# A two-layer backbone step: the second split pair of input projections taken half by half, and the bias load placed behind two weight loads

## What is computed

```python
sh1, sc1, g1, sh2, sc2, g2 = modulation(cond, w_ada[l], b_ada[l])   # silu(cond) @ w_ada, 6144 columns
h = rms_norm(x, norm1_g) * (1 + sc1) + sh1
proj = jnp.dot(h, w_in)
q_lat, ckv_raw, krope, conv_in, na_qkv = jnp.split(proj, IN_SPLITS, axis=-1)
...
s_loc = jnp.where(in_win, s_loc + bias, NEG_INF)    # neighbourhood attention, learned bias rpb
p = jax.nn.softmax(jnp.concatenate([s_loc, s_ctx], axis=-1), axis=-1)
...
x = x + g1 * jnp.dot(mix, w_out)
x = x + g2 * grouped_moe(h2, w_router, b_router, w_gate, w_up, w_down)
```

## Time and profile before

| | us |
|---|---|
| median of three runs | 1145.73 |
| lowest and highest run | 1142.65, 1146.65 |
| the profiled execution | 1150.03 |
| its span | 1148.2 |
| what lies around the span | 1.83 |

### The profile page before, as it was taken

How to read it: one execution, slowest core, us unless ns; L and a number is a source line. 1 busy time by engine, 2 the same in 40 slices (tenths; PEclk the granted TensorE clock), 3 DMA queues, 4 the chain that set the end, 5 groups by cost and what they waited for, 6 DMA issues and landing times.

```text
span 1148.2 us, 14862 instructions
## 1 busy us (share of the span) xinstructions
PE 1083.5 (94%) x5616; PEld 863.0 (75%) x5616; DVE 880.1 (77%) x1075; ACT 703.2 (61%) x927; POOL 227.0 (20%) x212
## 2 busy tenths in 40 slices
PE   5899799999899999999999999989889999999996
PEld 2677456588777888888878976778778888888884
DVE  1368554574899999998976688766689999899894
ACT  2334165553487887888855346653378788887880
POOL 2201411010323212212101033201215121221100
PEclk9899899989999999999999998969999999999998
DMA  9867696844689999999971323104599999999971
GB/s 380 321 257 278 199 378 263 312 187 170 263 340 361 356 394 377 375 389 378 388 296 53 112 106 106 48 1 202 196 345 375 355 389 380 382 357 378 379 290 56
DMA packets 54266, 320.63 MB, mean 279 GB/s; under 512 B 11610, under 2 KB 11722, under 8 KB 19248
## 3 DMA queue, kind: packets, MB, share of 16 engines
q1 hardware_dynamic: 38448, 276.59, 62.5%
q0 software_dynamic: 15744, 43.05, 10.1%
HBM read 313.37 MB, written 25.44 MB: 295 GB/s over the span
## 4 chain that ended last, share of the span: by engine, by line
PE 74%; DVE 15%; DMA 4%; ACT 3%; issue 3%; POOL 1%; SPq 0%; DVEq 0%; POOLq 0%; ACTq 0%
PE bank L1278 39%; PE bank L899 6%; PE bank L1170 5%; DVE w_lo L2436 5%; PE bank L917 4%; PE bank L882 3%; DMA ring<-wring_dram 3%; PE bank L994 3%; PE bank L1029 3%; PE bank L960 2%; PE bank L1270 2%; PE bank L927 1%; PE bank L1351 1%; PE bank L1307 1%; ACT probs L1564 1%
## 5 line engine op out<-in xcount | busy, mean ns | idle before, releaser
L2436 DVE TENSOR_TENSOR w_lo<-ring,w_hi 128x2048 fp32r<-128x2048 f32 x192 | 436.5, 2289 | 39.7 <-ACT w_hi L1715 39.6
L1715 ACT CAST w_hi<-ring 128x2048 fp32r<-128x2048 f32 x192 | 367.1, 1918 | 36.9 <-PE bank L1278 36.8
L1278 PE MATMUL bank<-w_hi,hgT_hi 128*128 128x512 f32 x512 | 202.3, 395 | 6.1 <-issue 4.2
L1278 PE MATMUL bank<-w_hi,hgT_lo 128*128 128x512 f32 x512 | 199.9, 391 | 0.0
L1278 PE MATMUL bank<-w_lo,hgT_hi 128*128 128x512 f32 x512 | 199.7, 390 | 0.0
L810 POOL DMA_INDIRECT y_rows<-y,y_at x26 | 48.2, 1852 | 354.4 <-ACT y L1746 325.4
L1278 PEld LDWEIGHTS bank<-w_hi,hgT_hi 128*128 128x128 f32 x512 | 96.2, 188 | 26.8 <-issue 7.7
L1278 PEld LDWEIGHTS bank<-w_hi,hgT_lo 128*128 128x128 f32 x512 | 96.1, 188 | 20.1
L1278 PEld LDWEIGHTS bank<-w_lo,hgT_hi 128*128 128x128 f32 x512 | 96.2, 188 | 19.2
L1278 PE MATMUL bank<-w_hi,hidT_hi 128*128 128x512 f32 x256 | 102.3, 400 | 0.0
L1278 PE MATMUL bank<-w_hi,hidT_lo 128*128 128x512 f32 x256 | 100.2, 391 | 0.0
(11 more groups left out here) (300 smaller groups left out, 1818.8 us busy)
## 6 DMA issues: line engine op xcount, KB each, us to landing
ring<-wring_dram SPq DMA_DIRECT2D x258, 1024.0 KB, 7.9
y_rows<-hg POOLq DMA_DIRECT2D x6, 1024.0 KB, 7.1
kT<-mod_dram POOLq DMA_DIRECT2D x4, 1024.0 KB, 7.4
late<-y_rows POOLq DMA_DIRECT2D x4, 1024.0 KB, 14.7
ring<-wring_dram SPq DMA_DIRECT2D x4, 832.0 KB, 10.6
h_rows<-h_tok POOLq DMA_DIRECT2D x6, 512.0 KB, 3.8
ring<-wring_dram SPq DMA_DIRECT2D x4, 640.0 KB, 9.4
bias<-na_bias_dram POOLq DMA_DIRECT2D x32, 64.0 KB, 6.8
```

The costliest lines, as they stand in the source:

```text
L1278: mm = pe.matmul(b[:, :], a, w[m], start=(start and k == 0), stop=(stop and k == 2))
L1715: act.copy(w_hi[:, q, :], in_ring(l, expert_slot(e, i))).then_inc(hi_made[q], 1)
L2436: dve.tensor_tensor(w_lo[:, q, :], in_ring(l, expert_slot(e, i)), w_hi[:, q, :], ALU.subtract) \
```

## The change

The second split pair is done by a new function. It takes the first slot through all three tiles, which leaves the sums in three banks open, and then the second slot through all three. Slot 26 (and its counterpart in layer 1) has a semaphore of its own, raised when the first slot has been used by the last tile; SP waits for it instead of the full bank. POOL waits, before the bias loads, until the second load of the pair before the heads (load 33) has landed. `pairs_after` is empty in layer 1, so POOL's new wait exists in layer 0 alone; the new order of products and the earlier release exist in both.

```diff
+    ... in_lo_made=4, first_slot_used=1,
@@ left(q)
                 stage = [js for js in STAGES if s - S_IN in js][0]
+                if s - S_IN == PAIRED[1][0]:
+                    return sems["first_slot_used"], nth(Layer(n), "first_slot_used", 1)
                 return once_full(Layer(n), ("proj", stage[0], TILES - 1))
@@ gpsimd
                 pool.wait_ge(*once_read(l, ("proj", 4, TILES - 1)))
+                for m, k in pairs_after(n, "heads"):
+                    pool.wait_ge(*once_loaded(Layer(m), 2 * k + 1))
@@ tensor
+            def project_pair_by_slots(l, i):
+                js, n = PAIRED[i], PAIR_WIDTH[i]
+                for h in range(2):
+                    pe.wait_ge(sems["in_lo_made"], nth(l, "in_lo_made", 2 * i + h + 1))
+                    for t in range(TILES):
+                        key = ("proj", js[0], t)
+                        if h == 0:
+                            pe.wait_ge(*once_free(l, key))
+                            pe.wait_ge(sems["hT_lo_made"], nth(l, "hT_lo_made", t + 1))
+                        b = bank[bank_no(l, key)]
+                        for c in range(4 * h, 4 * h + 4):
+                            cols = slice(c % 4 * n, (c % 4 + 1) * n)
+                            rows_hi, rows_lo = hT_hi[:, c, t * P:(t + 1) * P], hT_lo[:, c, t * P:(t + 1) * P]
+                            w_high, w_low = in_hi[:, h, cols], ring_lo[:, slot_turn(l, S_IN + js[h])[0], cols]
+                            for k, (a, w) in enumerate(((rows_hi, w_high), (rows_hi, w_low), (rows_lo, w_high))):
+                                mm = pe.matmul(b[:, 0:n], a, w, start=((c, k) == (0, 0)), stop=((c, k) == (KC - 1, 2)))
+                        if h == 1:
+                            mm.then_inc(bank_full[bank_no(l, key)], 1)
+                    if h == 0:
+                        mm.then_inc(sems["first_slot_used"], 1)
@@
-                project_pair(l, 1)
+                project_pair_by_slots(l, 1)
```

More of the change, by code:

```diff
@@ L148 @@
     meansq_ready=len(RMS), rstd_ready=len(RMS), normed_tile=TILES, latents_normed=1,
-    hT_hi_made=TILES, hT_lo_made=TILES, in_hi_made=4, in_lo_made=4,
+    hT_hi_made=TILES, hT_lo_made=TILES, in_hi_made=4, in_lo_made=4, first_slot_used=1,
     gate_sigmoid=1, glu_ready=1, conv_done=1, conv_silu=1, conv_high=1, conv_mixed=1, mix_high=TILES + 2,
```

## The result

| | before | after |
|---|---|---|
| median, 20 runs each, us | 1146.53 | 1138.23 |
| lowest and highest, us | 1141.74, 1152.89 | 1133.43, 1149.65 |
| profiled execution's span, us | 1148.2 | 1134.9 |
| PE's mean granted clock | 0.966 | 0.980 |

The ratio after to before is 0.9934, with a 95% interval of 0.9915 to 0.9952. That is 0.66% or 7.6 us faster, between 5.5 and 9.7. The forecast was 10.0 us and 1135.7 us, with a range of 1131.0 to 1142.0.

The account below looks back on a forecast made before the run. PE bounds the kernel (74% of the chain of waits), idling for late loads 32 and 33, then at half clock. Terms -3.0 - 3.7 - 3.7 + 0.5, taken as -10.0 us, took the median from 1145.73 to 1135.7 us, range 1131.0 to 1142.0.

Parts of the forecast that it names:

- POOL's wait: Layer 0, before the bias loads: POOL held to 128.4 us instead of 124.2, free well before its root is wanted; costs nothing.
- Layer 1: Layer 1's pair: no POOL wait and no hole before the transposes there, so nothing gained: 0.
- the open banks: The pair's 72 products: resuming banks in which sums stand taken as 0, with up to 0.7 us allowed.
- the later copies: After the pair's products: ACT's copies of the tiles come later, but the two that move are covered by ACT's idle time.
- The sum: Around loads 32, 33 and 38 in layer 0: -3.0 - 3.7 - 3.7 + 0.5 = -9.9, taken as -10.0 us.
- load 38's wait: At the scores behind load 38: it lands 1.4 us late, of which some 0.5 us comes through as a loss.
- the idling: PE's holes before loads 32 and 33, 3.04 and 4.03 us: only 0.3 us stays, so idling falls by 6.8 us.
- the clock term: PE's work behind the holes: granted clock stays at 1.00 instead of 0.50, returning 3.7 us.
- A: Rival, chance 0.20: the wait moves to the pairs of turns 1 and 2; gain 4 to 7 us, 1139 to 1142.
- C: Rival, chance 0.04: a mirrored hole at load 38 with a second clock fall makes it slower; 1150.4 if landing at 160.
- B: Rival, chance 0.06: load 33 takes 11.3 us again; only load 32's 3.0 us gained, 1142.7.
- D: Rival, chance 0.05: load 38 is in time and a later clock fall vanishes, more than forecast: 1132.

Follow-up runs that it names:

- e1: The changed kernel without POOL's wait, keeping the new product order and earlier slot release; median 1136.84 us, ratio 0.9907 to the kernel before.
- e5: The changed kernel with the old product order and old slot release in layer 1, so changed in layer 0 alone; ratio 0.9951 to the kernel before.
- e3: The kernel before with only the order of the 72 products changed, release and bias loads as before; median 1147.64 us, ratio 1.0015.
- e0: The changed kernel run and profiled once more; median 1136.78 us, ratio 0.9916 to the kernel before.
- b1: The kernel before, unchanged, in a second profile; no timed ratio, 117.7 us from issue of load 28 to load 57.
- b3: The kernel before, unchanged, in a fourth profile; no timed ratio, 118.0 us from issue of load 28 to load 57.
- b2: The kernel before, unchanged, in a third profile; no timed ratio, 118.0 us from issue of load 28 to load 57.
- e6: The changed kernel with layer 0's bias loads moved behind load 46 and the root for the second heads; median 1138.69 us, ratio 0.9945 to before.
- e8: The changed kernel with the first heads' transposes ahead of loads 32 and 33; median 1137.06 us, ratio 0.9932 to the kernel before.
- e9: The changed kernel with both the later layer-0 bias loads and the first heads' transposes ahead of loads 32 and 33; ratio 0.9929 to before.
- e2: The kernel before with only POOL's wait added, bias loads behind load 33, the pair still tile by tile; median 1142.32 us, ratio 0.9958.
- e4: The kernel before with ten spare 128-column products ahead of each of loads 32 and 33, no load moved; median 1140.61 us, ratio 0.9974.

## Why the prediction was right

**The mechanism** held at each step, but for two small waits that are named under the sum. The first half ends 8.3 us into the block; load 32 is there long before it is wanted; load 33 is the first of a burst and takes 4.8 us; the clock doesn't fall. POOL's wait costs nothing (and gives 0.3 us, e1), since its root for the second heads still follows 12.4 us of waiting for DVE. DVE still waits 3.06 us. Layer 1 gives nothing (the 73.2 us of e5), and neither the open banks nor the later copies cost anything to be seen (e3). One reading of the rows was loose: the fall began at 132.48, and up to there PE had idled for 4.28 of 5.35 us; the 8.1 us reach past it, to 135.26.

**The sum** of 10.0 us met the 10.1 of the same pair of profiles, with two errors that cancel. I had load 32's products follow at once, and missed that they open a bank which ACT must first empty: 0.80 us of waiting instead of 0.3 us for load 33. And I had 0.5 us of load 38's wait come through, where it was just in time: loads 35 to 38 land 4.3 us apart and not 4.75. Both are below the noise of a timed run. That they cancel is luck.

**The size** against the timed runs was high: 10.0 against 7.6 (5.5 to 9.7) and, in e0, 9.6 (6.5 to 12.7). The failing term is the idling. I took 3.04 + 4.03 us from one execution, in which load 32 and SP's issue of load 34 had been held up; the three later profiles have 4.5 to 5.0. Part of this was made good by the clock term, which was larger there than the 3.7 I put: this too was luck. With the place at 117.7 to 118.0 us before (b1 to b3) and 108.5 to 108.8 after (changed, e0, e1), a better size is 8.9 to 9.5 us. It isn't pinned down by four profiles, though. The side after is steady, from 108.0 to 108.8 us in all seven profiles with the early release. The side before hangs on how long the clock stays down: e3, which times like before, has 115.3, and with it the size would be 6.5 to 6.8 us.

**The other 3 us** of the spans are not the change's, as far as the profiles can tell. At load 28 the profile of the changed kernel is 1.9 us behind the first one of before; then it gains the 10.1 us to load 57, 2.7 us from 57 to 100 and 2.5 us from 163 to 180. From 57 to 100 it is the first profile of before that is long, with 189.7 us against 185.2 to 187.7 in b1 to b3 and 187.0 and 186.7 in the changed kernel. From 100 to 163 it is 219.2 us in every one of the 14 profiles. From 163 to 180, which holds the attention and the router of layer 1, long and short stretches stand on both sides:

| from load 163 to 180 | us | of these at a clock of 0.50, us |
|---|---|---|
| before, first profile; b1, b2, b3 | 222.7; 223.7, 222.9, 223.9 | 34.1; 30.7, 27.3, 30.7 |
| changed; e0 | 220.2; 218.5 | 20.5; 17.1 |
| e1, e6, e8, e9 | 222.0, 222.0, 222.6, 223.8 | 27.3, 27.3, 27.3, 30.7 |
| e3, e5 | 218.5, 218.4 | 17.1, 17.1 |
| e2, e4 | 219.9, 222.5 | 27.3, 27.3 |

e1 and e9 have the change and a long stretch; e3, whose timed ratio is 1.0015, and e5, which has the old order in layer 1, have a short one. The length mostly goes with the time that the clock spends at 0.50 (e2 is the exception), and so do the timed runs: of the 29 runs of before beside e0 to e3 the fastest, 1141.66 us, has a mean clock of 0.978 and the slowest, 1156.40 us, 0.961. One pair of spans couldn't have told 8 us from 13.

**The rivals.** A, a wait that moves behind the bias, is seen only at its edge: none, 0.16 and 0.48 us for load 38 in the three profiles of the change (the third is e5), and 0.80 in e2 and 0.96 (for load 40) in e8. It needed 3.5 to 6.5 us, load 38 landing at 151 to 154 where PE wants it at 147.5. Its price had left out the 1 us of slack that the sum and rival C use; with it the gain under A would have been 5 to 8 us and not 4 to 7. The Trainium skill's rule that the queues take turns packet by packet (DMA: Bandwidth & Descriptors, "Queues, rings and completion order") fits these profiles: with the bias in flight loads 34 to 37 of the changed kernel land 4.4 us apart, against 2.45 without. So does e6, where no bias is in flight: loads 35 to 38 land 2.5 us apart, against 4.3 in the changed kernel. But the consequence that I drew, that the bias's place doesn't matter, held only beside the early release, and for another reason than I gave: in e1 load 33 is issued 0.9 us ahead of the bias and is nearly through. Without the release (e2) the bias's place was worth 6.3 us of the place. B and C, a load 33 as late as before and a mirrored hole, did not come up in any profile with the early release (load 33 took 4.8 to 5.5 us). B's price was wrong as well. A load 33 that is issued at 123.6 and takes 11.3 us lands at 134.9, where it landed at 135.26 before. Load 32's 3.0 us would only have moved into the hole ahead of load 33, and the gain in idling would have been 0.4 us, not 3.0. D came in part: load 38 was nearly in time, and the fall at the second heads lasts 3.4 us in every profile of the change, against 3.4, 6.8, 6.8 and 6.8 in those of before. The timed median shows no more than the forecast.

What stays open: why load 32 was slow and SP's issue took 1.96 us in the first profile. POOL began to issue the bias just then, but it does so in b1 to b3 too, without the delay. No run tried to bring it about. Single slow issues occur elsewhere too (load 66 took SP 1.10 us in b3 and 1.30 in e5). Open is also why the clock is down for less long in e3's profile than in the four of before.

## What to carry to other kernels

A slot that is shared by several tiles should be released when the last tile has used it, and the loop order should make that moment early: here the release did all the work, and moving the competing traffic added 0.3 us on top, which no timing shows and which is within what two profiles of one kernel differ by. Price a hole in PE's work twice, once for its length and once for the work done at half clock behind it, and don't add two fixes that each close it. Before a size is taken from a transfer's duration in one execution, look for a sign that this execution was unusual (an issue six times its usual length), and measure a local gain between two fixed events, not between spans.

## What the runs showed of the hardware

- Three accumulation groups left open in three banks and resumed after 24 other products cost nothing to be seen: 16.64 us (changed) and 16.65 us (e3) for 72 products against 16.65.
- A load of 1,024 KB that is issued 0.9 us ahead of sixteen loads of 64 KB took 5.5 us instead of 4.8 (e1). One issued 0.4 us behind another such load and 0.5 us ahead of the same sixteen took 8.5 to 11.3 (before, b1 to b3, e3, e4), and 7.0 with the sixteen held back (e2).
- With those sixteen in flight, four loads of 1,024 KB landed 4.3 us apart; without them, 2.5 (changed, e6).
- Twenty spare products of 128 columns in two holes kept PE's clock at 2.4 GHz and were worth 3.0 us (0.5 to 5.4) of a kernel of 1145 us (e4). In b2, PE worked 9.20 us at 1.2 GHz behind the same holes.
